# Expert gathers of four slots by 32 tokens, summed by four 128x32 column tiles, in a hybrid decoder layer

## The reference

```python
x1 = layer_norm(alpha * x + mixer(x))
def one_block(xb):                       # 128 tokens
    q = (xb @ w_query).reshape(L, PEER_HEADS, 2, PEER_QUERY_DIM // 2)
    s = jnp.einsum('lhpd,hpkd->lhpk', q, sub_keys)
    vals, idx = lax.top_k(s, K)
    ...
    best, pos = lax.top_k(cand, K)
    expert = jnp.take_along_axis(cidx, pos, axis=-1)
    gate = jax.nn.softmax(best, axis=-1)
    u = expert_u[expert]
    v = expert_v[expert]
    h = jax.nn.gelu(jnp.einsum('ld,lhkd->lhk', xb, u), approximate=False)
    return jnp.einsum('lhk,lhkd->ld', h * gate, v)
x2 = layer_norm(alpha * x1 + one_block(x1))
```

## Time and profile before

| | us |
|---|---|
| three runs, median | 3737.79 |
| lowest to highest | 3734.94 to 3738.38 |
| profiled execution, span | 3737.1 |
| TensorE matmuls busy | 3095.8 (83%) |
| VectorE busy | 2162.5 (58%) |
| ScalarE busy | 1194.6 (32%) |
| GpSimd busy | 1178.9 (32%) |

### The profile page before, as it was taken

The page is one execution under the profiler, slowest core; times in us unless marked ns, Lnnn a source line. Parts: engine busy times, 40 slices in busy tenths (PEclk is TensorE's granted clock), DMA queues, the critical chain, the costliest instruction groups (busy, mean ns, idle before and its releaser), DMA issues.

```text
span 3737.1 us, 40978 instructions
## 1 busy us (share of the span) xinstructions
PE 3095.8 (83%) x11840; PEld 1827.3 (49%) x11840; DVE 2162.5 (58%) x5354; ACT 1194.6 (32%) x3475; POOL 1178.9 (32%) x1028
## 2 busy tenths in 40 slices
PE   7768977889779988789878998788987889777776
PEld 6555544555446545365444654455554555443222
DVE  4285557464674646746476554755556655575444
ACT  3115322353223532235212442235322353223222
POOL 0013333233232323324323243323423233333553
PEclk8789998999889999899988999899998999888999
DMA  6049988889898989889898898889988898889997
GB/s 267 23 190 346 363 353 349 322 338 364 345 360 327 350 347 350 347 322 359 334 364 348 315 391 333 327 353 345 377 345 337 330 351 351 359 318 364 417 420 331
DMA packets 174954, 1254.89 MB, mean 336 GB/s; under 512 B 20184, under 2 KB 20312, under 8 KB 23520
## 3 DMA queue, kind: packets, MB, share of 16 engines
q0 software_dynamic: 147456, 1073.81, 73.1%
q1 hardware_dynamic: 25056, 172.63, 11.8%
q10 hardware_dynamic: 2176, 5.36, 0.4%
HBM read 1247.53 MB, written 4.19 MB: 335 GB/s over the span
## 4 chain that ended last, share of the span: by engine, by line
PE 55%; DVE 21%; issue 9%; DMA 8%; ACT 6%; POOL 1%; DVEq 0%; POOLq 0%; ACTq 0%; SPq 0%
PE expert_sum L713 30%; PE bank L480 9%; DVE ring L1319 6%; DMA ring<-in_uv,expert_used 6%; PE bank L472 5%; PE bank L486 3%; DMA chunk<-in_weights 3%; DVE arena L1057 2%; PE bank L501 2%; DVE arena L1066 1%; DVE arena L1071 1%; DVE arena L1064 1%; ACT diag L929 1%; ACT h_raw L925 1%; DVE conv L1080 1%
## 5 line engine op out<-in xcount | busy, mean ns | idle before, releaser
L713 PE MATMUL expert_sum<-ring,diag 128*128 128x512 f32 x4096 | 1978.1, 632 | 532.5 <-ACT diag L929 529.8
L433 POOL DMA_INDIRECT ring<-in_uv,expert_used x1024 | 1178.7, 1151 | 2528.0 <-PE expert_sum L713 2170.1
L713 PEld LDWEIGHTS expert_sum<-ring,diag 128*128 128x128 f32 x4096 | 795.7, 202 | 1543.2 <-issue 988.5
L1319 DVE CUSTOM_DVE_ANT_0 ring<-ring,x_used 128x1024 f32<-128x1024 f32 x1024 | 1211.4, 1221 | 426.7 <-DMA ring<-in_uv,expert_used 392.1
L922 ACT ACTIVATE h_raw<-h_raw 128x2 f32<-128x2 f32 x512 | 104.0, 203 | 1502.2 <-DVE h_raw L1319 1501.9
L929 ACT ACTIVATE diag<-const,h_raw 128x128 f32<-128x128 f32 x1024 | 359.6, 394 | 38.3 <-PE expert_sum L713 36.7
L925 ACT ACTIVATE h_raw<-h_raw,gate_used 128x1 f32<-128x1 f32 x1024 | 245.6, 287 | 16.7
L1057 DVE MAX8 arena<-arena 128x8 f32<-128x128 f32 (+1 forms) x384 | 104.1, 326 | 229.4 <-ACT arena L902 214.9
L480 PEld LDWEIGHTS bank<-oT,chunk 128*128 128x128 f32 x1824 | 210.1, 193 | 15.3 <-issue 14.2
L480 PE MATMUL bank<-oT,chunk 128*128 128x128 f32 x1824 | 210.4, 277 | 0.7 <-ACT oT L892 0.7
L1080 DVE SCALAR_TENSOR_TENSOR conv<-conv_in,conv_w,conv 128x128 f32<-128x128 f32 x288 | 80.4, 345 | 186.8 <-ACT conv L770 186.8
(11 more groups left out here) (238 smaller groups left out, 2371.1 us busy)
## 6 DMA issues: line engine op xcount, KB each, us to landing
chunk<-in_weights SPq DMA_DIRECT2D x137, 1024.0 KB, 17.6
ring<-in_uv,expert_used POOLq DMA_INDIRECT x1024
ring<-in_weights SPq DMA_DIRECT2D x15, 1024.0 KB, 20.1
xT<-in_xT SPq DMA_DIRECT2D x8, 512.0 KB, 7.1
kept<-in_weights SPq DMA_DIRECT2D x4, 1024.0 KB, 11.3
x<-in_x SPq DMA_DIRECT2D x8, 512.0 KB, 9.5
out<-o_cat ACTq DMA_DIRECT2D x8, 512.0 KB, 8.0
sub_keys<-in_sub_keys ACTq DMA_DIRECT2D x1, 1024.0 KB
```

What stands on the lines that cost most here:

```text
L433: pool.indirect_dma_start(out=ring[:, (j % RING) * 2 * D:(j % RING + 1) * 2 * D], out_offset=None, in_=io["uv"], in_offset=bass.IndirectOf ...
L713: mm = pe.matmul(expert_sum[i][:, :], diag[:, (j % DIAGS) * P:(j % DIAGS + 1) * P], ring3[:, j % RING, D + i * 512:D + (i + 1) * 512], sta ...
L1319: dve.tensor_tensor_reduce(u, u, x1_used[:, :], 1.0, 0.0, ALU.mult, ALU.add, h_raw[:, j:j + 1]).then_inc(dotted.sem, 1)
```

## The change

A gather now fetches four slots for 32 tokens instead of one slot for 128. Partition 32s + t of gather 4q + c holds slot 4q + s of token 32c + t. Indices, gates and x1 are rearranged to fit, by 16 copies of 32 partitions each (`by_quad`; `x_quad` is four times as wide as `x1_used` was and holds each quarter of the tokens four times). The weights of a gather stand in a 128x32 matrix, four 32x32 diagonals under each other (`quarters`), so the product with the v half sums the four slots and gives 32 tokens. TensorE does the four gathers of a quad by four column tiles, each into its 32 partitions of `expert_sum`. There are 8 instead of 4 buffers of weights, three chunks kept instead of four, and `xT` lies in the place of `oT`. TensorE takes `(b - 1) // 2` quads where it took `b - 1` pairs.

```diff
+GROUPS = 4
+SPAN = P // GROUPS
+QUADS = SLOTS // GROUPS
-DIAGS = 4
-KEPT = 4
+DIAGS = 8
+KEPT = 3
...
+        "quarters": (i % SPAN) == np.arange(SPAN)[None, :],
...
-        xT = sb("xT", KT * P)
+        xT = oT
-        x1_used = sb("x1_used", D)
+        x_quad = sb("x_quad", GROUPS * D)
-        diag = sb("diag", DIAGS * P)
+        diag = sb("diag", DIAGS * SPAN)
...
             def experts(n, last):
-                for j in range(2 * taken[0], 2 * last):
-                    if j == 0:
+                for q in range(taken[0], last):
+                    if q == 0:
                         pe.wait_ge(*sums_read.at(n, 0))
-                    pe.wait_ge(*gathered[j % RING].at(n, arrived(j)))
-                    pe.wait_ge(*diag_ready.at(n, j + 1))
+                    for j in range(GROUPS * q, GROUPS * (q + 1)):
+                        pe.wait_ge(*gathered[j % RING].at(n, arrived(j)))
+                    pe.wait_ge(*diag_ready.at(n, GROUPS * (q + 1)))
                     for i in range(2):
-                        mm = pe.matmul(expert_sum[i][:, :], diag[:, (j % DIAGS) * P:(j % DIAGS + 1) * P],
-                                       ring3[:, j % RING, D + i * 512:D + (i + 1) * 512],
-                                       start=(j == 0), stop=(j == SLOTS - 1))
-                    mm.then_inc(added.sem, 1)
+                        for c in range(GROUPS):
+                            j = GROUPS * q + c
+                            mm = pe.matmul(expert_sum[i][c * SPAN:(c + 1) * SPAN, :],
+                                           diag[:, (j % DIAGS) * SPAN:(j % DIAGS + 1) * SPAN],
+                                           ring3[:, j % RING, D + i * 512:D + (i + 1) * 512],
+                                           start=(q == 0), stop=(q == QUADS - 1), tile_position=(0, c * SPAN))
+                            if i == 1:
+                                mm.then_inc(added.sem, 1)
...
-                mix(n, Marks(lambda a, b: experts(n - 1, b - 1)))
+                mix(n, Marks(lambda a, b: experts(n - 1, (b - 1) // 2)))
...
-                        act.activation(diag[:, (j % DIAGS) * P:(j % DIAGS + 1) * P], C["ident"], ACT.Copy,
+                        act.activation(diag[:, (j % DIAGS) * SPAN:(j % DIAGS + 1) * SPAN], C["quarters"], ACT.Copy,
                                        scale=h_raw[:, j:j + 1]).then_inc(diag_ready.sem, 1)
...
+            def by_quad(dst, src, first, last):
+                to = dst[:, first:last].rearrange("p (m c) -> p m c", c=GROUPS)
+                of = src[:, first:last].rearrange("p (m s) -> p m s", s=GROUPS)
+                for s in range(GROUPS):
+                    for c in range(GROUPS):
+                        ins = dve.tensor_copy(to[s * SPAN:(s + 1) * SPAN, :, c], of[c * SPAN:(c + 1) * SPAN, :, s])
+                return ins
...
-                dve.tensor_copy(expert_used[:, s], pos_hi[:, s]).then_inc(staged.sem, 1)
+                by_quad(expert_used, pos_hi, *s).then_inc(staged.sem, 1)
             def stage_rows(n):
                 dve.wait_ge(*chosen.at(n, 2))
-                dve.tensor_copy(gate_used[:, :], gate[:, :])
-                dve.tensor_copy(x1_used[:, :], x1[:, :]).then_inc(rows_staged.sem, 1)
+                by_quad(gate_used, gate, 0, SLOTS)
+                for s in range(GROUPS):
+                    for c in range(GROUPS):
+                        ins = dve.tensor_copy(x_quad[s * SPAN:(s + 1) * SPAN, c * D:(c + 1) * D], x1[c * SPAN:(c + 1) * SPAN, :])
+                ins.then_inc(rows_staged.sem, 1)
...
+                x_out = x_quad[:, 0:D]
                 for i in range(2):
-                    ins = stt(out=x1_used[:, i * 512:(i + 1) * 512], in0=x1_used[:, i * 512:(i + 1) * 512], scalar=ALPHA,
-                              in1=expert_sum[i][:, :], op0=ALU.mult, op1=ALU.add)
+                    for c in range(GROUPS):
+                        rows = slice(c * SPAN, (c + 1) * SPAN)
+                        ins = stt(out=x_out[rows, i * 512:(i + 1) * 512], in0=x_quad[rows, c * D + i * 512:c * D + (i + 1) * 512],
+                                  scalar=ALPHA, in1=expert_sum[i][rows, :], op0=ALU.mult, op1=ALU.add)
```

More of the change, by code:

```diff
@@ L63 @@
                       ("off64", P), ("same64", P), ("band", 2 * P), ("iota", TOPK),
-                      ("freq", HALF), ("eps_ln", 1), ("eps_rms", 1), ("eps_l2", 1), ("ln_qscale", 1)):
+                      ("freq", HALF), ("eps_ln", 1), ("eps_rms", 1), ("eps_l2", 1), ("ln_qscale", 1),
+                      ("quarters", P // 4)):
     CONSTS[_name] = (_at, _at + _width)
@@ L728, in _ @@
                 taken[0] = 0
-                mix(n, Marks(lambda a, b: experts(n - 1, b - 1)))
+                mix(n, Marks(lambda a, b: experts(n - 1, (b - 1) // 2)))
                 second_norm_rows(n)
-                experts(n - 1, PAIRS)
+                experts(n - 1, QUADS)
             taken[0] = 0
-            experts(NB - 1, RING)
+            experts(NB - 1, RING // 2)
             pe.wait_ge(*out_ready.at(NB - 2, 1))
             second_norm_rows(NB - 1)
-            experts(NB - 1, PAIRS)
+            experts(NB - 1, QUADS)
         @block.scalar
@@ L1294, in mix @@
                 mark("pick3")
+            def by_quad(dst, src, first, last):
[5 more added lines that the diff above has]
+                return ins
             def stage_first_ring():
-                dve.tensor_copy(expert_used[:, 0:RING], pos_hi[:, 0:RING]).then_inc(first_staged, 1)
+                by_quad(expert_used, pos_hi, 0, RING).then_inc(first_staged, 1)
             def stage_experts(n, part, start=0):
-                s = slice(start, STAGED) if part == 0 else slice(STAGED, SLOTS)
+                s = (start, STAGED) if part == 0 else (STAGED, SLOTS)
                 dve.wait_ge(*chosen.at(n, 1))
-                dve.tensor_copy(expert_used[:, s], pos_hi[:, s]).then_inc(staged.sem, 1)
+                by_quad(expert_used, pos_hi, *s).then_inc(staged.sem, 1)
             def stage_rows(n):
                 dve.wait_ge(*chosen.at(n, 2))
-                dve.tensor_copy(gate_used[:, :], gate[:, :])
-                dve.tensor_copy(x1_used[:, :], x1[:, :]).then_inc(rows_staged.sem, 1)
+                by_quad(gate_used, gate, 0, SLOTS)
[3 more added lines that the diff above has]
+                ins.then_inc(rows_staged.sem, 1)
             def experts(n, first, last):
@@ L1318, in experts @@
                         u = ring3[:, j % RING, 0:D]
-                        dve.tensor_tensor_reduce(u, u, x1_used[:, :], 1.0, 0.0, ALU.mult, ALU.add, h_raw[:, j:j + 1]).then_inc(dotted.sem, 1)
+                        dve.tensor_tensor_reduce(u, u, x_quad[:, (j % GROUPS) * D:(j % GROUPS + 1) * D], 1.0, 0.0, ALU.mult, ALU.add, h_raw[:, j:j + 1]).then_inc(dotted.sem, 1)
             def finish(n):
@@ L1336, in finish @@
                 dve.wait_ge(*stored.at(n, 0))
-                layer_norm(then_out, x1_used, LN2_G, LN2_B, ln2_rows.at(n, 1), ln2_rows.at(n, 2), o_cat, S_OUT, var_out, root_out.at(n, 1)).then_inc(out_ready.sem, 1)
+                layer_norm(then_out, x_out, LN2_G, LN2_B, ln2_rows.at(n, 1), ln2_rows.at(n, 2), o_cat, S_OUT, var_out, root_out.at(n, 1)).then_inc(out_ready.sem, 1)
                 dve.wait_ge(*out_ready.at(n, 1))
```

## The result

The changed kernel takes 3916.78 us (median of 4 runs, 3901.12 to 3920.86). The kernel before takes 3738.09 us beside it (4 runs, 3734.94 to 3743.17). The ratio is 1.047 (95% interval 1.0448 to 1.0494): slower by 4.7%. The forecast was 3600 and faster, its range 3470 to 3850. The time lies at rival B's 3910, but the trace shows that B's mechanism did not take place.

What follows compares the result with a forecast made beforehand. It took the bound to be a lockstep of TensorE and VectorE, with a transfer floor of some 372 us an iteration not far below. 3737.8 less 154 in the loop plus 17 outside gave 3600, range 3470 to 3850.

Steps and rivals of the forecast that it cites:

- rival B: Expert sum on TensorE: column tiles don't overlap, a quad costs 6.9 us; 3910, or 4060 if the ring empties; chance 0.20.
- When slots come free: Gather ring: slots freed four of eight at once; closing-part loop of 11.3 us fits in 12.5, so cost 0.
- The sum by stage: Loop iteration's five stages: 71, 114, 55, 146 and 46 us, together 432, 22 less than 454; seven times, -154.
- transfer floor: Least time for an iteration's transfers at 420 GB/s: some 372 us, with 108 in stage two and 138 in four.
- The expert sum: TensorE's sum over slots: two column tiles run at a time, a quad takes 3.4 us, the sum halves to 124 an iteration.
- A: Rival on TensorE: all four column tiles overlap, the expert sum falls to 62 us, time 3516; chance 0.20.
- Staging on VectorE: Between blocks: row copies 10.3 us, residual 4.1, gates 1.3, together 15.6 with nothing hiding it; index copies 0.
- The kept chunk: First stage, one kept chunk fewer: 2.5 us more transfer an iteration and up to 8.8 us of landing, from below 0.
- Rival C: Relief goes into another wait; lower TensorE clock stretches mixer matmuls from 134 to 167 us, giving 3715; chance 0.17.
- Chunk waits: Stage one: three chunk round trips fully paid make it 89 us, not 71, the iteration 450, the time 3727.

Runs made afterwards that it cites:

- pairs: Against the kernel before: gathers of two slots by 64 tokens, two 128x64 column tiles, slots freed by two, four chunks kept; 3606.43 us, ratio 0.9638.
- kernel with twelve slots: Changed kernel with one-copy staging (output mixes slots and tokens), no chunk kept, 12 ring slots instead of 8; 3521.08 us, ratio 0.9411 against the kernel before.
- doubled kernels: Each quad's matmuls issued twice: in the changed kernel, 4149.82 us; in quads with 12 slots, one-copy staging and no kept chunk, 3682.74 us.
- halved columns: Changed kernel with quads' matmuls 256 columns wide instead of 512, except a block's first and last quad; 3817.35 us, ratio 1.02 against the kernel before.

## Why the prediction was wrong, by its steps

**The step that failed is "When slots come free".** It took 0 for freeing by four. For the closing part it had 11.3 us against 12.5. With the three further landings of a quad (7.5 us) added on both sides, that is 18.8 us for two quads against the 20 in which eight gathers land. Measured are 22.6. By the rows these are 8.2 us from issue to first use (3713.44 to 3721.63), three more landings of 2.5, the dot's 1.2, ScalarE's 1.3, the quad's 3.6, and 0.8 from the last matmul to GpSimd's issue. So three terms were short: the latency was 5.4, a row of an idle queue, and is 8.2 with gathers ahead, the largest of them; the way back to GpSimd had no term (0.8); the quad was 3.4 for 3.6. That gives 11.3 us a quad; the window shows 4.19 MB at 380 GB/s, 11.0 us, where 10 would keep the rate of 420. One microsecond for some 30 quads, with 10.5 of the row copy and 4.3 of the residual, is the 46 us by which the closing part grew.

The step also looked at the closing part alone, and the larger loss is in the loop. There TensorE comes to a quad only at the written points of the mixer, one to two pairs late; two quads are all that eight slots hold, so one that waits takes half of the ring out of use. Made alone, with whole matmuls, freeing by four costs 540 us; with column tiles it costs some 180 against pairs, and four more slots win back 305.

**The sum by stage** fell with it. It predicted 71, 114, 55, 146 and 46 us; the stages last 71.8, 125.9, 51.1, 168.5 and 50.5. Of the 36 us between 432 and 468, stages two and four carry 34. There I had put both at the transfer floor plus a third of the idle time, as if TensorE's time had been the only reason for that idle. The DMA shares, 0.92 and 0.88, did not rise at all over the earlier trace rows.

The floor was set low besides. Length times DMA share makes 401 us of busy transfer engines in the iteration of the earlier trace rows and 398 in this one, where the rate of 420 GB/s gave 372. The kernel with twelve slots has a share of 0.93 in iterations of 420 us, 390 us busy. No run here came near 372.

**The expert sum.** "Two run at a time, not four" is refuted by the 16 records in 1.92 us. The 3.4 us for a quad came out by accident (3.64) where the clock is halved. The whole sum is 781 us busy, not near 1000. A's overlap happened, and A's 3516 did not.

**Staging on VectorE** was right in kind and place: +10.5 us for the rows (11.16 less the copy of 0.68), +3.0 for the gates and +4.3 for the residual, 17.8 for 15.6 predicted. The index copies, taken as 0, are 16 of some 168 ns twice a block; they and the boundary together measured 138 us over the run, where the prediction's terms give 8 times 15.6, 125. The opening grew by 14 us, of which the prediction had 13.

**The kept chunk** made the first stage 2 us longer in the sum, 14 in all; alone it measured 9.5. The first stage came out as forecast (71.8 for 71).

**Rival C's clock** was seen: 0.92 to 0.72 overall, 0.57 in the closing part. The mixer's matmuls, all but the expert sum, are busy 1361 us (2142.9 less 781.4) where they were 1118, 244 us more or some 30 a block, near the 33 an iteration that C worked out. How much of that lies on the path stays open. The doubled kernels were granted more and lost time, and twelve slots reach 421 GB/s at a clock of 0.59, so the half clock doesn't hold back the closing part once slots are there. How much of the 99 us of halved columns belongs to the clock wasn't separated. **Chunk waits** of the kind that C named are there but smaller than its 18 us an iteration: 43 us in all before L477 and 30 before L485, some 10 an iteration, where the kernel before had 12 us in all.

**Rival B** gave the number and not the reason, which is luck. It decided by a pitch of 0.43 us, one tile at a time, with a quad of 6.9 us; that did not occur. Its "first slot of a quad freed later" was the right worry, attached to the wrong condition.

What stays open: how the cost of freeing by four, in either form, splits between waiting for the fourth slot and TensorE's lag behind the dot products. Less lag alone made another wait of it (4396 us), and no kernel here separates the two.

## What to carry to other kernels

When a change makes an engine's work cheaper by grouping it, price the group first as a hold on buffers: with N places and groups of g only N/g groups are in flight, and the loop must be counted from the first issue to the last member's use, with latencies of a loaded queue. Try the smallest group that gives the packing (pairs gave 3.6%, where quads lost 4.7%), and spend memory on places before anything else once groups are used. A test with more places tells cheaply whether a fall in throughput is a shortage of places: 305 us here, and no net gain in the kernel before.

## What of the hardware was unexpected

- Four 128x32 column tiles in fp32 overlap wholly: 16 records of 512 columns in 1.92 us at full clock, 3.64 at half clock.
- Making TensorE's work sparser lowers its granted clock, here from 0.92 to 0.72 on average and to 0.50 with halved columns in the closing part. The mean record of the expert sum lasts 903 ns in the changed kernel (clock 0.72) and 836 with twelve slots (0.751).
- A copy of 32 partitions by 1024 columns takes 685 ns, as long as one of 128 partitions (682 to 687).
- A gather into a queue with others ahead takes 8.2 us from issue to use, against 5.4 into an idle one.
- The busy share of the DMA engines can stand at 0.98 while they move 380 GB/s; at 1.01 they moved 420. The share alone does not tell that they are kept fed.
